# Hybrid attention and convolution layer on one core: a second accumulator bank, output weights in sixteen pieces, a reordered last tile, and side work placed behind the scores

## The chip, the cores and the metric

The kernel runs on one core of one Trainium2 chip. The metric is device time in microseconds (us); lower is better. Three runs of the kernel before gave 764.88, 765.08 and 765.8 us, so its median is 765.08 us.

## The reference

```python
h = rms_norm(x, norm_w)
proj = einsum('bsd,de->bse', h, w_in)
q, kv_all, gate_logits, nsa_z, cv_h, cv_b, cv_c, cv_z = split(proj)
# 8 heads x 64, 2 key groups, three branches, each a masked softmax over its own keys
o_cmp = softmax(q k_c) v_c      # 64 compressed blocks (a small MLP over 32 tokens each)
o_slc = softmax(q k_s) v_s      # all causal tokens: 16 blocks of 64 are all selected at SEQ = 1024
o_win = softmax(q k_w) v_w      # sliding window of 512
o_nsa = (g0 * o_cmp + g1 * o_slc + g2 * o_win) * silu(nsa_z)
u = cv_c * cv_h
o_conv = cv_b * (causal_conv_3(u) + conv_b) * silu(cv_z)       # 512 channels
out = x + concat([o_nsa, o_conv]) @ w_out                      # 1024 x 1024
```

SEQ is 1024 and the model width 1024, all in float32. The kernel keeps float32 accuracy by splitting both operands of a product into a high part in the type fp32r and a rest, and takes three products of 128 x 128 by 128 x 512 (`three`: high x high, high x low, low x high).

## The kernel before, in words

The first 200 us or so normalise x, and project queries, keys, values and a part of the gates. The change doesn't touch them. After that one loop over 136 steps (numbered k, in the code `for k in range(STEPS)`) interleaves two streams of work on TensorE.

**The attention stream.** A unit is a query tile i (128 queries, i = 0 to 7) and a key group g. It has two jobs, the selected branch ("s", even jobs) and the window branch with the compressed one ("w" and "c", odd jobs), and each job has four heads, so there are 128 score steps. Step k writes, at its end, the scores of step k+1 (`scores`, lines 1260 to 1285) into one of two tiles `sc[k % 2]` of two banks each. It must wait until the exponentials of step k-1 have been read from that tile (`exp_done`). VectorE takes the row maxima (lines 1095 to 1099), ScalarE the exponentials (779 to 784), VectorE, ScalarE and GpSimd scale by gate and sum. From step 4n+5 on, the probabilities of job n are transposed on TensorE (`turn`, line 1401), ScalarE casts them to a high part (`pth`, 794), VectorE takes the rest (`ptl`, 1106), and the products with the values follow one turn later (`flush`, 1381 and 1382). The rows grow with i, from 128 to 1024 columns. Every eight steps the next unit's queries are transposed (1249) and split (704, 966).

**The side stream.** It has 52 groups of eight parts, one part being three products of 512 columns. Groups 0 to 35 compute the gate and convolution channels (kinds z, ch, cc, cb, cz, each for two column halves); groups 36 to 51 are the output projection, two for each query tile. Before, all groups but the last accumulate in one bank, `pf`. A group's first part waits until the one before has been read from `pf` (`f_free`, an ordinary counter). How it is read depends on the kind: z is a tanh on ScalarE (762) and then a product on VectorE (1044); ch is a copy on ScalarE (765); cc is a product on VectorE (1052), and after its second half a pass of ScalarE over 1024 columns (768) and two of VectorE (1068, 1069, `convolve`); cb is a product on VectorE (1056); cz is a tanh and two VectorE instructions (1059, 1061); an output group is added to x (1115) and stored.

**The order.** `SIDE` says for each step how many parts lie in its first and in its second group of parts. One step on TensorE is: first turn (or flush), first group of parts, second turn, second group of parts, scores of k+1, queries. The other engines walk through the same steps in the same written order, so an instruction that waits holds up all that stands behind it on its engine.

**The output weights.** w_out (1024 x 1024) is loaded by SP in eight pieces of 128 x 1024 into two buffers `wor0` and `wor1`, cast by ScalarE (831), and its rest taken by GpSimd for even pieces (565) and by VectorE for odd ones (1155), in steps 88 to 91. The last channel part stands in step 87, step 88 has no parts, and steps 89 to 92 have one part in each group. An output part needs its piece (`wol_ready`).

**The last tile.** Query tile 7's output, parts 400 to 415, takes four parts of column half 0, four of half 1, and the same again with the attention half of the mix, which ScalarE casts (837) and GpSimd takes the rest of (570) once both key groups are done.

Of the kernel before, what the change touches and what calls it, by code (L numbers as in the profile page):

```python
# [15 lines left out]
P = 128  # L16
# [71 lines left out]

def win_column(i):
    return 512 - min(i, WT) * P  # L90
# [26 lines left out]

SIDE = [(2, 2)] * 34 + [(2, 1), (2, 1), (2, 0)] * 18 + [(0, 0)] + [(1, 1)] * 4  # L120
# [36 lines left out]

OUT_0 = 8 * NF
# [26 lines left out]
def mixn_half_at(k):  # L185

    for m in range(NT):
        if step_of(OUT_0 + 16 * m + (4 if m == LAST else 0)) == k:
            return m
    return None  # L190
# [5 lines left out]

def wout_at(k):

    return [j for j in range(NK) if WOUT_STEP + j // 2 == k]
# [16 lines left out]
def hybrid_layer(nc: bass.Bass, x, wpack, wside, wout, normw, qnorm, knorm, par, const, maskc, out):  # L216
    with ExitStack() as ctx:
# [26 lines left out]
        with ExitStack() as c:  # L244
# [21 lines left out]
            with ExitStack() as d:  # L266
                wor = [sb("wor0", [P, DM], F32, d), None]
                msh = sb("msh", [P, NK, P], F32R, d)
                msl = sb("msl", [P, NK, P], F32R, d)
                wor[1] = sb("wor1", [P, DM], F32, d)  # L270
# [9 lines left out]
                with ExitStack() as f:  # L280
                    xo = [sb(f"xo{s}", [P, 512], F32, f) for s in range(2)]
# [35 lines left out]
        f_done, f_free, f_tanh, cz_done = sem("f_done"), sem("f_free"), sem("f_tanh"), sem("cz_done")  # L317
        conv_first, conv_done = sem("conv_first"), sem("conv_done")
        wor_in = [sem(f"wor_in{s}") for s in range(2)]
        woh_ready = sem("woh_ready")  # L320
        wol_ready = [sem(f"wol_ready{s}") for s in range(2)]
# [6 lines left out]
        msh_ready, msl_ready = sem("msh_ready"), sem("msl_ready")  # L328
        out_done, out_ready, mixc_used = sem("out_done"), sem("out_ready"), sem("mixc_used")
# [63 lines left out]
        def side_bank(x):  # L393

            return sc[0][:, 0:512] if x == NX - 1 else pf[:, :]
# [14 lines left out]
        def _(sp):  # L410
# [50 lines left out]
            for j in range(NK):  # L461
                output_weights(j)
                if j == 1:
                    sp.wait_ge(conv_done, 4)
                    for c in range(2):
                        residual(c)
# [12 lines left out]
        def _(pool):  # L479
# [66 lines left out]
            for k in range(STEPS):  # L546
# [33 lines left out]
        def _(act):  # L580
# [171 lines left out]
            def side(f):  # L752
# [3 lines left out]
                if kind in ("z", "cz"):  # L756
                    act.wait_ge(f_done, f + 1)
                    if kind == "cz":
                        before = 2 * t + f % 2
                        if before:  # L760
                            act.wait_ge(cz_done, before)
                    A(th[:, :], pf[:, :], ACT.Tanh, scale=0.5).then_inc(f_tanh, 1)
                elif kind == "ch":
                    act.wait_ge(f_done, f + 1)
                    nc.scalar.copy(mixc[:, t, cols], pf[:, :]).then_inc(f_free, 1)
                elif kind == "cc" and f % 2 == 1:
                    act.wait_ge(f_free, f + 1)
# [3 lines left out]
            def exponentials(s):  # L771
# [9 lines left out]
                else:  # L781
                    A(cmp_probs(i, h), sc[s % 2][:, 640:704], ACT.Exp,
                      bias=nmax[:, s % 4, 1:2], accum_out=psums[:, s % 4, 1:2])
                    A(win_probs(i, h), sc[s % 2][:, win_column(i):512 + P], ACT.Exp,
# [15 lines left out]
            for k in range(STEPS):  # L800
# [27 lines left out]
                for j in wout_at(k):  # L828
                    act.wait_ge(wor_in[j % 2], 16 * (j // 2 + 1))
# [656 lines left out]
```

## Time and profile before

| | before |
|---|---|
| median of three runs | 765.08 us |
| profiled execution | 767.03 us |
| its span in the trace | 765.2 us |
| TensorE busy | 702.6 us (92%) |
| VectorE, ScalarE, GpSimd busy | 459.1, 372.9, 189.1 us |
| mean granted TensorE clock | 0.986 |

The span is the time from the first to the last instruction of the profiled execution; 1.8 us more lie around it. TensorE is busy nearly all the time, so a gain has to come from the moments in which it is idle, or runs at a lower clock. The end of a matmul in the trace is modelled: a product of 512 columns is shown with 0.39 us, yet the next one starts 0.23 us later. Start times are therefore the better measure.

### The profile page before, as it was taken

To read this page: it belongs to the slowest core of one execution; us is meant where nothing else is said; L and a number is where in the kernel's file an instruction comes from. 1 tells how busy PE (TensorE), PEld (TensorE's weight loads), DVE (VectorE), ACT (ScalarE), POOL (GpSimd) and SP (SyncE) were. 2 spreads that over 40 slices of the span, in tenths; PEclk is the share of its full clock that TensorE was granted. 3 is DMA by queue.
4 is the path that set the end of the run, shared out by engine and by line. 5 is a ranking of instruction groups with operands and counts; after the bars stand their busy time and mean duration, and the time that the engine had idled before them with its cause. 6 is when DMAs were issued, how large, how long until landed. Compare 5 with 4: busy or idle time off the path is not lost.

```text
span 765.2 us, 10923 instructions
## 1 busy us (share of the span) xinstructions
PE 702.6 (92%) x3951; PEld 588.7 (77%) x3951; DVE 459.1 (60%) x957; ACT 372.9 (49%) x896; POOL 189.1 (25%) x209
## 2 busy tenths in 40 slices
PE   1989999799989999999999999999779999999997
PEld 1878899698768778877877787787557878887775
DVE  3777453734333644567568666687657676776742
ACT  4552525432333434446555555555565555555541
POOL 2112545320223222132122122120341121202120
PEclk9999999999999999999999999999979999999999
DMA  6521131201111101110111000002131111110101
GB/s 207 166 84 28 31 108 38 80 1 42 29 41 42 29 27 42 29 42 15 28 28 28 15 29 28 14 4 80 55 110 42 43 41 42 35 50 28 56 28 56
DMA packets 18053, 36.75 MB, mean 48 GB/s; under 512 B 2512, under 2 KB 3408, under 8 KB 18000
## 3 DMA queue, kind: packets, MB, share of 16 engines
q1 hardware_dynamic: 18000, 36.05, 15.2%
q8 instruction: 32, 0.52, 0.3%
q14 instruction: 21, 0.17, 0.1%
HBM read 31.85 MB, written 4.19 MB: 47 GB/s over the span
## 4 chain that ended last, share of the span: by engine, by line
PE 70%; DVE 13%; ACT 6%; issue 6%; DMA 4%; POOL 1%; SPq 0%; POOLq 0%; ACTq 0%; DVEq 0%
PE pf L1167 11%; PE pf L1168 10%; PE pf L1169 10%; PE tp L1401 6%; PE pj L1167 5%; PE pj L1168 5%; PE pj L1169 4%; PE po L1381 4%; PE po L1382 4%; PE sc L1258 4%; PE sc L1257 3%; DMA wor<-in_wout 2%; DMA qp<-in_wpack 1%; DVE ptl L1106 1%; DVE wol L1155 1%
## 5 line engine op out<-in xcount | busy, mean ns | idle before, releaser
L794 ACT CAST pth<-tp 128x512 fp32r<-128x512 f32 (+1 forms) x148 | 86.5, 586 | 146.1 <-PE tp L1401 145.9
L1106 DVE TENSOR_TENSOR ptl<-tp,pth 128x512 fp32r<-128x512 f32 (+1 forms) x148 | 101.8, 688 | 53.6 <-ACT pth L794 51.1
L1167 PE MATMUL pf<-hh,fh 128*128 128x512 f32 x288 | 116.8, 406 | 7.6 <-DVE mixn L1044 4.6
L1168 PE MATMUL pf<-hl,fh 128*128 128x512 f32 x288 | 112.7, 391 | 0.0
L1169 PE MATMUL pf<-hh,fl 128*128 128x512 f32 x288 | 112.6, 391 | 0.0
L552 POOL TENSOR_SCALAR qp<-qp,precip,gate 128x64 f32<-128x64 f32 x64 | 39.7, 621 | 215.6 <-DVE precip L1081 215.6
L1401 PE MATMUL tp<-cst,qp 128*128 128x128 f32 (+1 forms) x592 | 90.5, 276 | 1.4 <-issue 1.1
L510 POOL TENSOR_TENSOR fl<-fraw,fh 128x512 fp32r<-128x512 f32 x36 | 46.8, 1299 | 150.1 <-ACT fh L661 150.1
L1167 PE MATMUL pj<-wh,hh 128*128 128x256 f32 (+1 forms) x256 | 75.9, 296 | 6.7 <-POOL wl L493 5.4
L1095 DVE TENSOR_REDUCE nmax<-sc 128x1 f32<-128x128 f32 (+7 forms) x64 | 48.4, 756 | 47.2 <-PE sc L1276 46.9
L1168 PE MATMUL pj<-wl,hh 128*128 128x256 f32 (+1 forms) x256 | 74.2, 290 | 0.0
L1167 PEld LDWEIGHTS pf<-hh,fh 128*128 128x128 f32 x288 | 54.1, 188 | 26.1 <-DVE mixn L1044 5.2
L1169 PE MATMUL pj<-wh,hl 128*128 128x256 f32 (+1 forms) x256 | 74.1, 289 | 0.0
L1401 PEld LDWEIGHTS tp<-cst,qp 128*128 128x128 f32 (+1 forms) x592 | 67.2, 139 | 8.5 <-issue 2.4
L1381 PE MATMUL po<-pth,val 128*128 128x512 f32 x132 | 64.2, 486 | 8.8 <-DVE ptl L1106 5.7
L493 POOL TENSOR_TENSOR wl<-qp,wh 128x512 fp32r<-128x512 f32 (+1 forms) x33 | 45.8, 1414 | 92.2 <-ACT wh L592 92.1
L1169 PEld LDWEIGHTS pf<-hh,fl 128*128 128x128 f32 x288 | 54.1, 188 | 12.2
L1168 PEld LDWEIGHTS pf<-hl,fh 128*128 128x128 f32 x288 | 54.1, 188 | 10.6
L1167 PE MATMUL pf<-woh,msh 128*128 128x512 f32 x120 | 49.8, 415 | 8.1 <-POOL wol L565 6.4
L1087 DVE TENSOR_SCALAR qp<-qp,precip,gate 128x640 f32<-128x640 f32 (+7 forms) x96 | 55.1, 574 | 3.5
L1167 PEld LDWEIGHTS pj<-wh,hh 128*128 128x128 f32 x256 | 50.3, 196 | 9.0 <-issue 7.7
L1257 PE MATMUL sc<-kst,qh 128*128 128x512 f32 (+3 forms) x152 | 52.5, 346 | 1.1 <-DVE ql L966 1.1
(179 smaller groups left out, 1522.0 us busy)
## 6 DMA issues: line engine op xcount, KB each, us to landing
fraw<-in_wside SPq DMA_DIRECT2D x36, 256.0 KB, 2.7
qp<-in_wpack SPq DMA_DIRECT2D x28, 256.0 KB, 3.0
qp<-in_x SPq DMA_DIRECT2D x8, 512.0 KB, 3.4
wor<-in_wout SPq DMA_DIRECT2D x8, 512.0 KB, 4.3
xo<-in_x SPq DMA_DIRECT2D x16, 256.0 KB, 2.7
out<-xo SPq DMA_DIRECT2D x16, 256.0 KB, 2.0
qp<-in_wpack SPq DMA_DIRECT2D x5, 224.0 KB, 2.6
mixc<-in_normw SPq DMA_DIRECT2D x1, 512.0 KB, 7.5
```

Source lines behind the costliest of these rows:

```text
L493: nc.gpsimd.tensor_tensor(wl[e % 2][:, j * w:(j + 1) * w], raw[p % 4][:, 0:w], wh[e % 2][:, j * w:(j + 1) * w].bitcast(F32), ALU.subtract)\
L510: nc.gpsimd.tensor_tensor(fl[h % 3][:, :], fraw[h % 2][:, :], fh[h % 3][:, :].bitcast(F32), ALU.subtract)\
L794: nc.scalar.copy(pth[ptn % 2][0:r, :], tp[tpn % 2][0:r, :]).then_inc(pth_ready, 1)
L1087: V.tensor_scalar(p, p, factor, main, ALU.mult, ALU.mult).then_inc(p_dve, 1)
L1095: V.tensor_reduce(nmax[:, s % 4, 0:1], sc[s % 2][:, o:o + (i + 1) * P], AX.X, ALU.max, negate=True).then_inc(max_ready, 1)
L1106: V.tensor_tensor(ptl[ptn % 2][0:r, :], tp[tpn % 2][0:r, :], pth[ptn % 2][0:r, :].bitcast(F32), ALU.subtract).then_inc(tp_read, 1)
L1167: MM(dst, lh, rh, start=start, stop=False)
L1168: MM(dst, lh, rl, start=False, stop=False)
L1169: return MM(dst, ll, rh, start=False, stop=stop)
L1257: MM(dst, qh[:, h, :], keys, start=True, stop=False)
L1381: MM(po[:, :], v, pth[pt % 2][0:r, :], start=first, stop=False)
L1401: ins = nc.tensor.transpose(tp[tpn % 2][0:r, h * P:(h + 1) * P], src, ident)
```

## The change

- **A second side bank.** Odd groups below group 23 (1, 3, ... 21) accumulate in the upper half of `sc[0]`, a bank of its own, and so does group 51. The window scores of tiles 0 to 2 are moved down into the lower half (`end_column`). Each bank counts its own readers (`f_free[bank]`, `uses`), and a group waits only for the last one in its own bank. The scores of step 52 (`WIDE_STEP`), the first wide window row, wait for groups 21 and 22.
- **The order of a step.** The second group of parts now follows the scores of k+1 instead of standing before them.
- **SIDE.** Full steps (2, 2) go on two steps longer, the channels end in step 86 (first group of parts), the step without parts is 87, and eight steps (88 to 95) with (1, 1) follow in place of four (89 to 92). The number of parts is the same.
- **Output weights.** Sixteen pieces of 128 x 512 in four buffers, two per step in steps 87 to 94; ScalarE casts each and GpSimd takes the rest of each. VectorE has none left. The first residual tiles are loaded after the last channel group.
- **Last tile.** Six parts of column half 0, six of half 1, then the last two of each. The attention half of the mix is cast in two quarters, in steps 131 and 133, and VectorE takes their rest instead of GpSimd.

```diff
+def end_column(i):
+    return 512 if i >= 3 else i * P
 def win_column(i):
-    return 512 - min(i, WT) * P
+    return end_column(i) - min(i, WT) * P
...
-SIDE = [(2, 2)] * 34 + [(2, 1), (2, 1), (2, 0)] * 18 + [(0, 0)] + [(1, 1)] * 4
+SIDE = [(2, 2)] * 36 + [(2, 1), (2, 1), (2, 0)] * 17 + [(0, 0)] + [(1, 1)] * 8
...
+WIDE_STEP = next(k for k in range(NS) if k // 4 % 2 and end_column(UNITS[k // 8][0]) == 512)
+EARLY = (SIDE_AT[2 * (WIDE_STEP - 2)]) // 8
+def bank_of(x):
+    return int(x < EARLY and x % 2 == 1 or x == NX - 1)
+def uses(x):
+    return sum(bank_of(y) == bank_of(x) for y in range(x))
...
     if m == LAST:
-        k, n = part // 8 * 4 + part % 4, part // 4 % 2
+        n, k = (part // 6, part % 6) if part < 12 else ((part - 12) // 2, 6 + part % 2)
...
+LAST_STEPS = (output_step(2 * LAST) + 6, output_step(2 * LAST + 1))
 def wout_at(k):
-    return [j for j in range(NK) if WOUT_STEP + j // 2 == k]
+    return [j for j in range(2 * NK) if WOUT_STEP + j // 2 == k]
+def wout_piece(j):
+    n, k = divmod(j, NK)
+    return KT_ORDER[k], slice(n * 512, (n + 1) * 512)
...
         def side_bank(x):
-            return sc[0][:, 0:512] if x == NX - 1 else pf[:, :]
+            return sc[0][:, 512:1024] if bank_of(x) else pf[:, :]
+        def bank_free(eng, x):
+            eng.wait_ge(f_free[bank_of(x)], uses(x) + 1)
...
             def output_weights(j):
-                k = KT_ORDER[j]
+                k, cols = wout_piece(j)
                 if j == 0:
-                    sp.wait_ge(f_done, NF - 2)
-                elif j == 1:
+                    sp.wait_ge(conv_done, 4)
+                elif j == 2:
                     sp.wait_ge(fl_ready, NHALF)
-                else:
-                    sp.wait_ge(wol_ready[j % 2], j // 2)
-                sp.dma_start(wor[j % 2][:, :], wout[k * P:(k + 1) * P, :]).then_inc(wor_in[j % 2], 16)
+                elif j >= 4:
+                    sp.wait_ge(wol_ready, j - 3)
+                sp.dma_start(wor[j % 4][:, :], wout[k * P:(k + 1) * P, cols]).then_inc(wor_in[j % 4], 16)
...
                 for j in wout_at(k):
-                    if j % 2 == 0:
-                        kt = KT_ORDER[j]
-                        pool.wait_ge(woh_ready, j + 1)
-                        nc.gpsimd.tensor_tensor(wol[:, kt, :], wor[0][:, :], woh[:, kt, :].bitcast(F32), ALU.subtract)\
-                            .then_inc(wol_ready[0], 1)
+                    kt, cols = wout_piece(j)
+                    pool.wait_ge(woh_ready, j + 1)
+                    nc.gpsimd.tensor_tensor(wol[:, kt, cols], wor[j % 4][:, :], woh[:, kt, cols].bitcast(F32), ALU.subtract)\
+                        .then_inc(wol_ready, 1)
...
                 for j in wout_at(k):
-                    act.wait_ge(wor_in[j % 2], 16 * (j // 2 + 1))
+                    kt, cols = wout_piece(j)
+                    act.wait_ge(wor_in[j % 4], 16 * (j // 4 + 1))
                     act.wait_ge(f_done, NF)
-                    nc.scalar.copy(woh[:, KT_ORDER[j], :], wor[j % 2][:, :]).then_inc(woh_ready, 1)
+                    nc.scalar.copy(woh[:, kt, cols], wor[j % 4][:, :]).then_inc(woh_ready, 1)
...
+                if k in LAST_STEPS:
+                    g = LAST_STEPS.index(k)
+                    dve.wait_ge(last_hi, g + 1)
+                    V.tensor_tensor(msl[:, 2 * g:2 * g + 2, :], mixn[:, 2 * g:2 * g + 2, LAST * P:],
+                                    msh[:, 2 * g:2 * g + 2, :].bitcast(F32), ALU.subtract).then_inc(last_lo, 1)
...
+                if k == WIDE_STEP:
+                    bank_free(pe, EARLY - 1)
+                    bank_free(pe, EARLY - 2)
...
-                if k == 0 and f >= 1:
-                    pe.wait_ge(f_free, f)
+                if k == 0 and uses(f):
+                    pe.wait_ge(f_free[bank_of(f)], uses(f))
...
                 for t in turned[1:]:
                     turn(n, *t)
+                if k + 1 < NS:
+                    scores(k + 1)
                 for p in side_parts(k, 1):
                     channels(p) if p < OUT_0 else output(p)
-                if k + 1 < NS:
-                    scores(k + 1)
```

## Rows read from the trace of the kernel before

**Rows 1.** The page, sections 1 and 2: busy time, then 40 equal slices in tenths.

```profile
PE 702.6 (92%) x3951; PEld 588.7 (77%) x3951; DVE 459.1 (60%) x957; ACT 372.9 (49%) x896; POOL 189.1 (25%) x209
...
PE   1989999799989999999999999999779999999997
...
PEclk9999999999999999999999999999979999999999
```

**Rows 2.** TensorE's waits: who waited, for whom, us in total, times, longest.

```profile
PE po L1381 <- DVE ptl L1106: 7.9, 9, 3.6
PE pf L1167 <- POOL wol L565: 6.4, 2, 3.2
PE pf L1167 <- DVE mixn L1044: 4.6, 4, 1.2
...
PE pf L1167 <- DVE th L1059: 1.7, 5, 0.5
```

**Rows 3.** Timeline, group 0 to 1: start, duration, engine, line, operation, [idle before].

```profile
204.97 0.23 PE L1276 MATMUL sc<-maskb 128*128 128x128 bf16 x1
...
206.36 0.50 PE L1167 MATMUL pf<-hh,fh 128*128 128x512 f32 x1 [1.17 <-DVE mixn L1044]
```

**Rows 4.** Timeline: scores, then parts of the same group (209); scores, then a turn (235).

```profile
209.41 0.23 PE L1276 MATMUL sc<-maskb 128*128 128x128 bf16 x1
209.45 0.47 PE L1167 MATMUL pf<-hh,fh 128*128 128x512 f32 x1
...
209.76 0.40 PE L1168 MATMUL pf<-hl,fh 128*128 128x512 f32 x1
...
235.45 0.23 PE L1276 MATMUL sc<-maskb 128*128 128x128 bf16 x1
...
235.52 0.61 PE L1401 MATMUL tp<-cst,qp 128*128 128x128 f32 x4
```

**Rows 5.** Timeline, first convolution: group 7's end, its exponentials, next queries, next unit's scores.

```profile
257.43 0.25 PE L1257 MATMUL sc<-kend,qh 128*128 128x192 f32 x1
...
259.80 0.35 ACT L784 ACTIVATE qp<-sc,nmax 128x128 f32<-128x128 f32 x1
...
264.45 0.68 DVE L966 TENSOR_TENSOR ql<-tp,qh 128x512 fp32r<-128x512 f32 x1
...
265.19 0.39 PE L1257 MATMUL sc<-kst,qh 128*128 128x256 f32 x1 [0.30 <-DVE ql L966]
```

**Rows 6.** Timeline: the last channel group is read (step 87); TensorE's next product with values.

```profile
540.76 0.60 ACT L762 ACTIVATE th<-pf 128x512 f32<-128x512 f32 x1
...
546.43 0.79 PE L1381 MATMUL po<-pth,val 128*128 128x512 f32 x1 [3.60 <-DVE ptl L1106]
```

**Rows 7.** Two stretches: us, busy by engine (instructions), PEclk, DMA share, GB/s.

```profile
556.60:563.00 6.40, 6.34 (x18) 4.78 (x19) 3.85 (x6) 4.66 (x8) 4.48 (x5) 0.50 0.51 164
...
577.00:589.50 12.50, 12.50 (x72) 10.21 (x71) 8.39 (x19) 7.78 (x20) 2.41 (x3) 1.00 0.13 43
```

**Rows 8.** Groups by line and shape: busy us, mean ns | idle before, releaser.

```profile
L510 POOL TENSOR_TENSOR fl<-fraw,fh 128x512 fp32r<-128x512 f32 x36 | 46.8, 1299 | 150.1 <-ACT fh L661 150.1
...
L661 ACT CAST fh<-fraw 128x512 fp32r<-128x512 f32 x36 | 22.4, 621 | 26.7 <-PE pf L1169 26.6
```

**Rows 9.** The tile `wor`: ns minimum/median/maximum, first and last start, forms.

```profile
L565 POOL TENSOR_TENSOR wol<-wor,woh x4: 2343/2362/2387, 547.2 to 568.6; 128x1024 fp32r<-128x1024 f32 x4
L1155 DVE TENSOR_TENSOR wol<-wor,woh x4: 1228/1477/2643, 548.1 to 570.7; 128x1024 fp32r<-128x1024 f32 x4
```

**Rows 10.** Timeline: a GpSimd subtraction and a VectorE scaling at the same time.

```profile
401.17 1.27 POOL L510 TENSOR_TENSOR fl<-fraw,fh 128x512 fp32r<-128x512 f32 x1 [5.87 <-ACT fh L661]
...
401.39 1.33 DVE L1087 TENSOR_SCALAR qp<-qp,precip,gate 128x512 f32<-128x512 f32 x1
```

**Rows 11.** Timeline, last tile: cast of the mix, and the first part that needs it.

```profile
754.25 0.62 ACT L837 CAST msh<-mixn 128x512 fp32r<-128x512 f32 x1 [1.39 <-DVE mixn L1141]
...
756.26 0.50 PE L1167 MATMUL pf<-woh,msh 128*128 128x512 f32 x1 [1.22 <-POOL msl L570]
```

More of the change, by code:

```diff
@@ L185, in mixn_half_at @@
 def mixn_half_at(k):
-    for m in range(NT):
-        if step_of(OUT_0 + 16 * m + (4 if m == LAST else 0)) == k:
+    for m in range(LAST):
+        if step_of(OUT_0 + 16 * m) == k:
             return m
@@ L266, in hybrid_layer @@
             with ExitStack() as d:
-                wor = [sb("wor0", [P, DM], F32, d), None]
+                xo = [sb(f"xo{s}", [P, 512], F32, d) for s in range(2)]
                 msh = sb("msh", [P, NK, P], F32R, d)
                 msl = sb("msl", [P, NK, P], F32R, d)
-                wor[1] = sb("wor1", [P, DM], F32, d)
+                wor = [None, None] + [sb(f"wor{s}", [P, 512], F32, d) for s in (2, 3)]
                 qd = sb("qd", [P, GH, 2, HD], F32, d)
@@ L280, in hybrid_layer @@
                 with ExitStack() as f:
-                    xo = [sb(f"xo{s}", [P, 512], F32, f) for s in range(2)]
+                    wor[0], wor[1] = (sb(f"wor{s}", [P, 512], F32, f) for s in (0, 1))
         with ExitStack() as c:
@@ L316, in hybrid_layer @@
         fh_ready, fl_ready, half_used = sem("fh_ready"), sem("fl_ready"), sem("half_used")
-        f_done, f_free, f_tanh, cz_done = sem("f_done"), sem("f_free"), sem("f_tanh"), sem("cz_done")
+        f_done, f_tanh, cz_done = sem("f_done"), sem("f_tanh"), sem("cz_done")
+        f_free = [sem(f"f_free{s}") for s in range(2)]
         conv_first, conv_done = sem("conv_first"), sem("conv_done")
-        wor_in = [sem(f"wor_in{s}") for s in range(2)]
-        woh_ready = sem("woh_ready")
-        wol_ready = [sem(f"wol_ready{s}") for s in range(2)]
+        wor_in = [sem(f"wor_in{s}") for s in range(4)]
+        woh_ready, wol_ready = sem("woh_ready"), sem("wol_ready")
         qd_ready, qh_ready, kend_ready = sem("qd_ready"), sem("qh_ready"), sem("kend_ready")
@@ L451, in output_weights @@
             def output_weights(j):
[L452 removed]
+                k, cols = wout_piece(j)
                 if j == 0:
[L454 to L455 removed]
+                    sp.wait_ge(conv_done, 4)
+                elif j == 2:
                     sp.wait_ge(fl_ready, NHALF)
[L457 to L461 removed]
+                elif j >= 4:
+                    sp.wait_ge(wol_ready, j - 3)
+                sp.dma_start(wor[j % 4][:, :], wout[k * P:(k + 1) * P, cols]).then_inc(wor_in[j % 4], 16)
+            for j in range(4):
                 output_weights(j)
[L463 to L466, printed above, removed]
+            sp.wait_ge(f_done, NF)
+            for c in range(2):
+                residual(c)
+            for j in range(4, 2 * NK):
+                output_weights(j)
             for c in range(2 * NT):
@@ L757, in side @@
                     act.wait_ge(f_done, f + 1)
[L758 to L762, printed above, removed]
+                    if kind == "cz" and 2 * t + f % 2:
+                        act.wait_ge(cz_done, 2 * t + f % 2)
+                    if kind == "z" and f >= 1:
+                        bank_free(act, f - 1)
+                    A(th[:, :], side_bank(f), ACT.Tanh, scale=0.5).then_inc(f_tanh, 1)
                 elif kind == "ch":
                     act.wait_ge(f_done, f + 1)
-                    nc.scalar.copy(mixc[:, t, cols], pf[:, :]).then_inc(f_free, 1)
+                    nc.scalar.copy(mixc[:, t, cols], side_bank(f)).then_inc(f_free[bank_of(f)], 1)
                 elif kind == "cc" and f % 2 == 1:
-                    act.wait_ge(f_free, f + 1)
+                    bank_free(act, f - 1)
+                    bank_free(act, f)
                     A(mixc[:, t, :], ub[:, 2:2 + SEQ], ACT.Identity, scale=prm[:, P_CW + 3 * t + 2:P_CW + 3 * t + 3],
@@ L1043, in side @@
                     dve.wait_ge(f_tanh, f + 1)
-                    V.scalar_tensor_tensor(mixn[:, t, cols], th[:, :], 1.0, pf[:, :], ALU.add, ALU.mult).then_inc(f_free, 1)
+                    V.scalar_tensor_tensor(mixn[:, t, cols], th[:, :], 1.0, side_bank(f), ALU.add, ALU.mult)\
+                        .then_inc(f_free[bank_of(f)], 1)
                 elif kind == "cc":
@@ L1277, in scores @@
                 else:
-                    o, j0 = win_column(i), max(0, i - WT)
+                    o, e, j0 = win_column(i), end_column(i), max(0, i - WT)
                     if j0 < i:
-                        keys_times(s[:, o:512], kst[:, 1, g, j0 * P:i * P], h, i < WT)
-                    keys_times(s[:, 512:512 + P + CB], kend[:, g, :], h, False)
+                        keys_times(s[:, o:e], kst[:, 1, g, j0 * P:i * P], h, i < WT)
+                    keys_times(s[:, e:e + P + CB], kend[:, g, :], h, False)
                     if i >= WT:
                         MM(s[:, 0:P], identb, farb, start=False, stop=True)
-                    ins = MM(s[:, 512:512 + P + CB], identb, endb[:, i, :], start=False, stop=True)
+                    ins = MM(s[:, e:e + P + CB], identb, endb[:, i, :], start=False, stop=True)
                 ins.then_inc(s_done, 1)
```

49 lines of the change are left out of this document (28 added, 21 removed).

## The prediction

> **What bounds the kernel now.** I read the busy shares first. TensorE is busy 92% of the span, no other engine above 60%, and the slices show where the rest lies: the start, one slice near 540 to 575 us where both its busy share and its clock fall to 7 tenths, and a thin loss elsewhere [rows 1]. The change leaves the first 200 us alone. Then I read TensorE's own list of waits, which gives the thin loss its names: a channel group waiting until VectorE has read the bank (lines 1044, 1059), parts of the output waiting for the rest of w_out, and value products waiting for `ptl` [rows 2]. Last I read the timeline at one instance of each. So TensorE sets the time nearly everywhere after 200 us, and each edit is worth what it takes from, or adds to, the gaps between TensorE's starts.
>
> **Part 1: the second bank.** Between group 0 and group 1 TensorE ends its scores at 204.97 and starts the next part at 206.36, 1.39 us [rows 3]. Where the same order has no change of group the step is 0.04 us [rows 4]. The stall is worth 1.35 us, while the list of waits books 1.17, because matmul ends are modelled. Four z boundaries cost 4 x 1.33 = 5.3 us. The other 18 boundaries up to group 22 cost 0 to 0.7 us each (on line 1059, cz, five waits of 1.7 us in all, [rows 2]), by the same reading of starts 5.7 us. The second bank removes all 22 waits, since the group before the previous one has long been read: -11.0 us. The lower end is what the list of waits books for them, some 7.6.
>
> Part of it comes back. With scores(k+1) before the second group of parts, TensorE reaches them 1.38 us (two parts of six products, 0.23 each) earlier, and after a group has ended, ScalarE must first read that group and then take the exponentials that these scores wait for. For z and ch that is 0.6 us plus 0.5 to 0.9, against 1.38 to 1.74 us of parts and turn on TensorE: nearly hidden, I take +0.5 us in total. For the two convolutions in this stretch it isn't hidden. Group 7's products end at 257.43, its exponentials at 260.15, and the next queries are ready at 265.13 because VectorE is in `convolve` until then; the next unit's scores start right behind, 7.8 us after the group's end [rows 5]. That chain runs on ScalarE and VectorE and doesn't shorten. After the change TensorE has one set of scores and two parts less to do inside it (1.7 us), and must do two parts behind it. Laid out step by step, TensorE passes the end of that step 1.3 us later than before, and 1.4 us later at the second convolution (group 15), the bank waits there not gained. Against the 11.0 us, which counts those four boundaries as gained, this is +3.4 us. The later convolutions keep their cover: 0.
>
> **Part 2: the order costs TensorE something of itself.** Scores end in a bf16 product with the mask. Scores followed by a part cost 0.04 us to the next start and 0.31 us for the part's first product, where 0.23 is usual; scores followed by a turn cost 0.07 us [rows 4]. The new order makes scores, part, turn out of part, scores, turn in each step that has a second group and a turn or queries behind it: 82 steps by SIDE. That is 0.04 + 0.08 - 0.07 = 0.05 us each, 82 x 0.05 = +4.1 us. It could be 0 (if the turn behind the part gains what the part loses) or 0.10 each, 8 us.
>
> **Part 3: the output weights.** Before, from the read of the last channel group (540.76) to the end of step 95 (589.5) pass 48.7 us [rows 6, 7]. TensorE's work in it, at the usual distances, is 16 parts x 0.69 = 11.0, 12 turns with their value products x 0.91 = 10.9, nine scores x 0.78 = 7.1 and one set of queries 0.4, in all 29.4 us. The other 19.3 us are waits (3.60 and twice 3.2 us as the longest, [rows 2, 6]) and the half clock behind each: after such a wait the granted clock reads 0.50 for 3 to 6 us, and TensorE does 18 products in 6.4 us where it does 72 in 12.5 at full clock [rows 7]. That is its 1.2 GHz level instead of 2.4.
>
> After, the last channel group ends one step earlier, so 3.0 us more of TensorE's work (two turns, one set of scores, queries) stand behind that point: 32.4 us of work. The waits that remain: at the drain, ScalarE's tanh, two VectorE passes and the cast of the mix still stand before the exponentials, so the scores of step 88 wait about 1.1 us, the first output part 0.7 (its piece's cast and rest are 0.62 and 1.30 us, [rows 8]) and the next value product 0.5. None is as long as the 3.6 us, so I expect the clock to stay up. Then two pieces per step: ScalarE was busy 7.78 us in the three steps 93 to 95, 2.6 a step [rows 7], and 2 x 0.62 more make 3.8, while TensorE's step with two parts is (12.5 - 2 x 0.69) / 3 = 3.7. GpSimd comes to 2 x 1.30 + 0.8 = 3.4, VectorE 2.8. So ScalarE is level with TensorE for seven steps and lags after steps with two turns: I lay out 3.4 us of small waits. Loads don't matter: 256 KB pieces, four buffers, each asked for two steps ahead. And VectorE's scaling on line 1087 (0.61 us on average) takes 1.33 us when a GpSimd subtraction runs beside it [rows 10]; with GpSimd busy most of each step I add 1.3 us. That gives 32.4 + 2.3 + 3.4 + 1.3 = 39.4 us, against 48.7 + 3.0 = 51.7: -12.3 us. Bounds: -17 if only the drain remains, -8 if the 3.6 us wait and its half clock survive.
>
> The row says more here than the mean: the GpSimd subtraction of 1024 columns takes 2.36 us, VectorE's 1.23 at its fastest and 1.48 in the median [rows 9]. The Trainium skill, "GPSIMD Engine Reference", section 4.1 (Engine selection), says that two-input elementwise work belongs on VectorE, as GpSimd is about twice as slow, and this change does the opposite. The trace agrees with the factor; by that rule the stage would end bound by GpSimd, which is the first rival below.
>
> **Part 4: the last tile.** TensorE stands idle 1.22 us (1.38 by starts) until GpSimd has taken the rest of the attention half [rows 11]. After, 12 parts don't need the last key group, so four more (2.8 us) lie behind the cast at 754.25, and the quarter's cast and rest take about 0.8 us together. The wait goes, and the parts behind it are the same in number: -1.4 us, at worst 0.
>
> **Part 5: where group ends fall.** SIDE moves most channel ends by one step. Four waits of 0.4 to 1.4 us in the steps 60 to 84 came from a group's end standing before `ptl` or before the read of the value product on its engine (of [rows 2], line 1381); I count 3.6 us gone and 1.6 new: -2.0, between +2 and -3.6.
>
> **Sum.** -11.0 + 3.4 + 0.5 + 4.1 - 12.3 - 1.4 - 2.0 = -18.7 us. The profiled execution took 767.03 us, its span 765.2 with 1.8 around it, so a span of 746.5. The median of the runs shown lies 1.95 below the profiled execution; the same difference taken off its 765.08 gives 746.4, and I predict 746.5.
>
> **Rivals.**
>
> - **GpSimd and ScalarE take the weights stage back.** If GpSimd is slowed by its neighbour as VectorE was, whose same instruction took 1.2 times its fastest in the median and 2.2 times at worst [rows 9], say by 1.4, a piece takes 1.8 us instead of 1.3; sixteen make 29 us, 5 us of other work come to it, and eight steps of 3.7 are 30: GpSimd bound, 34 against 30. With ScalarE lagging as well, TensorE waits some 4 to 7 us more: 752. For it: the equal loads above. Against it: 1.30 us is the mean of 36 of the same form [rows 8], and the four on line 565 hardly differ [rows 9]. Chance 0.17.
> - **The earlier scores wait.** The second bank does nothing but move the wait: TensorE gets past the group's end and stops at the scores, whose exponentials stand behind the same read. Half of the 11 us returns, and the order costs 0.10 us a step instead of 0.05: 746.5 + 4 + 4 = 754.5. For it: the convolution [rows 5]. Against it: in the list of TensorE's waits none stands on an exponential at all. Chance 0.13.
> - **The other side: slower.** One mechanism: the scores stop for the exponentials of step k-1 in every step with a second group, not only behind group ends, because ScalarE's queue runs level with TensorE. It takes 0.23 us more in each of the 82 steps to eat 18.7 us; at 0.25 the time is 767. ScalarE is at 49%, so I give it 0.03.
> - **The weights stage without residue**: all small waits hidden and the alignment good, -17 and -3.6 in place of -12.3 and -2.0: 740. Chance 0.12.
>
> The forecast keeps 0.55. The range 737 to 755 holds the forecast and the first, second and last of these. A difference of 0.2% is about what a measurement of this kernel can tell from none. Faster by more than that 0.95, within it 0.02, slower 0.03.
>
> **What would show each step.** Waits of line 1167's channel parts on VectorE for groups 1 to 22 gone from the list. Starts after the mask product at 0.04 and 0.31 us. The next unit's scores still 7.8 us behind group 7's end, with 2 to 3 us of waits before them. Granted clock 1.0 through the weights stage, and about 39 us from the last channel group's end to the end of step 95. No wait before the last four parts. The prediction is wrong if the clock still halves there, or if scores wait on exponentials outside the convolutions.

## The result, and the profile after

The changed kernel takes 752.88 us (median of four runs, 752.47 to 753.7), against 764.98 us for the kernel before in the same comparison (four runs, 762.55 to 765.8): ratio 0.9848, interval 0.9824 to 0.9873. It is faster by 12.1 us, inside the range forecast, but 6.4 us short of the 746.5 us predicted.

First the page of the changed kernel, the lines that answer [rows 1].

```profile
PE 699.6 (93%) x3951; PEld 582.8 (78%) x3951; DVE 461.3 (61%) x955; ACT 372.8 (50%) x905; POOL 198.1 (26%) x220
...
PE   2899999799999899999999999999899999999997
...
PEclk9999999999999999999998999999999999999999
```

The hole near 540 to 575 us is nearly gone (8 and 9 tenths where it read 7), and its clock is whole again. The one slice whose clock falls to 8 tenths is now at 394 to 413 us; experiment 4 goes there. None of the other engines is near its limit, since VectorE, the busiest of them, stands at 61%. TensorE's waits after 205 us, in the columns of [rows 2]:

```profile
PE po L1434 <- DVE ptl L1158: 5.6, 8, 1.4
PE sc L1308 <- ACT qp L825: 3.2, 4, 1.4
PE sc L1308 <- DVE ql L1014: 2.5, 2, 1.5
PE pf L1218 <- POOL wol L604: 2.1, 3, 1.3
...
PE tp L1454 <- issue: 1.8, 1, 1.8
```

The waits of channel parts on lines 1044 and 1059 have gone and the wait for the weights' rest fell from 6.4 to 2.1 us. Scores that wait for exponentials (line 825) are a new name. One turn waits 1.8 us for a releaser that the list doesn't know ("issue"); before, the longest wait of that kind was 1.1 us. The first is the forecast's, the second isn't.

**One measure for all kernels.** The profiled spans are 765.2 and 750.7 us, 14.5 us apart, more than the medians are, because the part ahead of the loop, which no edit touches, varies by some us from one execution to the next (its end stands at 204.97 and 202.16 us). So I compare the distance in the trace from the first scores' mask product to the start of the last product. Before it is 204.97 [rows 3] to 761.61, 556.6 us. The timeline of the changed kernel:

```profile
202.16 0.23 PE L1330 MATMUL sc<-maskb 128*128 128x128 bf16 x1
...
747.03 0.39 PE L1220 MATMUL sc<-woh,msl 128*128 128x512 f32 x1
```

That is 544.9 us, 11.8 less, in agreement with the medians. Each distance is read from one execution, so differences of a few tenths say little. All kernels by this measure ("usual order" is the scores last in a step, as before):

| kernel | distance | median | ratio to before (interval) |
|---|---|---|---|
| before | 556.6 | 764.98 | 1 |
| changed | 544.9 | 752.88 | 0.9848 (0.9824 to 0.9873) |
| changed, usual order | 534.9 | 744.33 | 0.9714 (0.9681 to 0.9747) |
| changed, one bank | 557.0 | 766.65 | 1.0023 (0.9999 to 1.0047) |
| changed, late convolutions | 540.4 | 749.42 | 0.9788 (0.9757 to 0.9818) |
| before, new order | 569.1 | 778.99 | 1.0165 (1.0118 to 1.0213) |
| before, two banks | 545.9 | 755.50 | 0.9857 (0.9818 to 0.9895) |
| best: changed, usual order, late convolutions | 531.1 | 739.92 | 0.9649 (0.962 to 0.9679) |
| best, VectorE takes odd pieces' rest | 534.7 | 743.43 | 0.9705 (0.9667 to 0.9744) |
| best, last tile as before | 532.7 | 740.92 | 0.9664 (0.9634 to 0.9694) |
| best, eight weight blocks | 542.7 | 750.89 | 0.9807 (0.9784 to 0.983) |
| changed, usual order in twelve steps | 540.0 | 747.39 | 0.9782 (0.9735 to 0.9829) |

### The profile page after: what moved, and what is told of

Its sections match the earlier page's. It is cut to its first block, busy times and chain, and to the rows that moved or that the text cites. A ratio compares the mean times of both kernels' runs of the same rounds, so it can differ in the third digit from the quotient of the medians.

```text
span 750.7 us, 10966 instructions
## 1 busy us (share of the span) xinstructions
PE 699.6 (93%) x3951; PEld 582.8 (78%) x3951; DVE 461.3 (61%) x955; ACT 372.8 (50%) x905; POOL 198.1 (26%) x220
## 4 chain that ended last, share of the span: by engine, by line
PE 76%; DVE 11%; ACT 5%; issue 4%; POOL 2%; DMA 2%; SPq 0%; ACTq 0%; DVEq 0%; POOLq 0%
PE pf L1218 10%; PE pf L1220 9%; PE pf L1219 9%; PE tp L1454 7%; PE po L1434 5%; PE pj L1218 5%; PE pj L1219 5%; PE pj L1220 5%; PE sc L1308 4%; PE sc L1309 4%; PE po L1435 4%; PE sc L1218 3%; PE sc L1220 3%; PE sc L1219 3%; DVE ptl L1158 1%
## 5 line engine op out<-in xcount | busy, mean ns | idle before, releaser
L1218 PE MATMUL pf<-hh,fh 128*128 128x512 f32 x200 | 85.2, 426 | 0.6 <-DVE ub L1101 0.6
L1454 PEld LDWEIGHTS tp<-cst,qp 128*128 128x128 f32 (+1 forms) x592 | 71.2, 138 | 18.7 <-issue 3.3
L1219 PE MATMUL pf<-hl,fh 128*128 128x512 f32 x200 | 79.1, 395 | 0.0
L1220 PE MATMUL pf<-hh,fl 128*128 128x512 f32 x200 | 79.0, 395 | 0.0
L1138 DVE TENSOR_SCALAR qp<-qp,precip,gate 128x640 f32<-128x640 f32 (+7 forms) x96 | 58.5, 609 | 3.5
L1146 DVE TENSOR_REDUCE nmax<-sc 128x1 f32<-128x128 f32 (+7 forms) x64 | 48.3, 754 | 12.7 <-PE sc L1330 12.5
L1309 PE MATMUL sc<-kst,ql 128*128 128x512 f32 (+3 forms) x152 | 52.4, 347 | 0.0
L1435 PE MATMUL po<-ptl,val 128*128 128x512 f32 x132 | 52.1, 395 | 0.0
L1219 PEld LDWEIGHTS pj<-wl,hh 128*128 128x128 f32 x256 | 49.7, 194 | 0.0
```

What stands on the lines that cost most here:

```text
L1138: V.tensor_scalar(p, p, factor, main, ALU.mult, ALU.mult).then_inc(p_dve, 1)
L1146: V.tensor_reduce(nmax[:, s % 4, 0:1], sc[s % 2][:, o:o + (i + 1) * P], AX.X, ALU.max, negate=True).then_inc(max_ready, 1)
L1218: MM(dst, lh, rh, start=start, stop=False)
L1219: MM(dst, lh, rl, start=False, stop=False)
L1220: return MM(dst, ll, rh, start=False, stop=stop)
L1309: MM(dst, ql[:, h, :], keys, start=False, stop=stop)
```

## The experiments

**1. The order of a step.** Theory: the new order costs time and gives none back. Rival: it is what makes the bank useful. First it is undone alone in the changed kernel (label x1), then done alone in the kernel before (x4).

```diff
-                if k + 1 < NS:
-                    scores(k + 1)
                 for p in side_parts(k, 1):
                     channels(p) if p < OUT_0 else output(p)
+                if k + 1 < NS:
+                    scores(k + 1)
```

> The changed kernel with the second group of parts ahead of the scores again, all else as changed. My theory: the new order costs 0.05 us of TensorE in each of 82 steps (4.1 us), and gives back part of the second bank's gain at the two early convolutions (about 3 us), so this version takes 745 to 747 us, against 752.9. The waits of the scores on ScalarE's exponentials go, and the wait of 1.85 us at step 53 (third convolution) stays, since that comes from where the convolution stands on VectorE. Rival: the earlier scores give the other engines slack that pays for the order; then this version takes 753 to 757 us. Second rival, for step 53 alone: the order causes that wait; then step 53 takes 5.4 us instead of 8.5.

> The kernel before with one edit: the second group of parts follows the scores. My theory: 4.1 us for the switch from mask product to part in 82 steps, 5 to 7 us because the waits at the channel groups' boundaries lose the scores that lay in them, 2 to 3 us at the two early convolutions: 776 to 779 us. Rival: the order is worth something by itself (scores earlier, so more slack for the other engines); then it takes 760 to 768 us.

Measured: 744.33 us and 778.99 us. The second lies in the theory's range, the first 0.7 us below it, so the order costs a little more than the theory had; the rival falls in both. The wait at step 53 stays with the usual order, even longer (2.56 us for 1.85), so the second rival falls as well. By distance the order costs 10.0 us with two banks and 12.5 us with one. In neither does it bring a gain.

**2. The bank.** In the changed kernel all groups but the last go back to one bank (x2, the edit below). In the kernel before the second bank comes alone, by the change's own hunks on `bank_of`, `end_column` and `f_free`, with the order, the side work and the weights as they were (x6).

```diff
 def bank_of(x):
-    return int(x < EARLY and x % 2 == 1 or x == NX - 1)
+    return int(x == NX - 1)
```

> The changed kernel with all side groups but the last in the one bank pf; new order, weights and last tile stay. My theory: the 22 waits at the channel groups' boundaries come back, and each is longer by the scores that no longer lie behind it (0.2 to 0.5 us), less what TensorE spends waiting at the two early convolutions anyway: 13 to 17 us, so 766 to 770 us. Rival: the second bank only moved the wait from the part to the scores; then this version takes 756 to 760 us.

> The kernel before with the second bank alone (steps of fewer than eight groups): order, side work and weights as before. Theory: the waits for the bank at the group boundaries of the first 23 groups go, 11.0 us in the sum of the prediction, and the first two convolutions, which then run with less time ahead of them, take part of it back: 764.9 - 8 to 10 = 755 to 757 us. Rival: the bank brings nothing without the new order, because the side group between a mask product and the first part moves the wait to the scores or to the mask product: 762 to 765 us.

Measured: 766.65 us, and 755.5 us. The bank is worth 10.7 us by distance in the usual order (556.6 to 545.9) and 12.1 us in the new one (557.0 to 544.9). The second figure is too low, because the changed kernel's profiled execution holds a stretch at half clock that the one-bank kernel's doesn't (experiment 4); the medians are 13.8 us apart. The bank doesn't need the new order. What it removes is seen in the waits of TensorE from 205 to 320 us, first before:

```profile
PE pf L1167 <- DVE mixn L1044: 4.6, 4, 1.2
PE pf L1167 <- DVE th L1059: 0.9, 2, 0.5
PE pf L1167 <- DVE ub L1052: 0.5, 1, 0.5
PE pf L1167 <- DVE mixc L1056: 0.4, 1, 0.4
PE sc L1257 <- DVE ql L966: 0.3, 1, 0.3
```

and before with two banks, where the scores' wait for the next queries at the two early convolutions (1.0 us each) is all that is left. With one bank these two are 0.3 us, in the list above, and 0.8 us at 329.62, behind its end; so the two convolutions take back 0.9 us even in the usual order:

```profile
PE sc L1287 <- DVE ql L992: 2.0, 2, 1.0
```

**3. Where the order's cost sits.** The changed kernel with the usual order in steps 12 to 17 and 28 to 33 alone (x10), the steps around the first two convolutions.

```diff
+                early = not (12 <= k < 18 or 28 <= k < 34)
-                if k + 1 < NS:
+                if early and k + 1 < NS:
                     scores(k + 1)
                 for p in side_parts(k, 1):
                     channels(p) if p < OUT_0 else output(p)
+                if not early and k + 1 < NS:
+                    scores(k + 1)
```

> The changed kernel with the old order in twelve of its steps alone, 12 to 17 and 28 to 33, around the first two convolutions. It tests where the new order costs its 8.5 us: in waits at the early convolutions, or evenly. Theory: the waits there fall by 1.8 and 2.0 us (as they did with the old order everywhere), and twelve switches at 0.04 us each go: 752.9 - 4.3 = 748.6 us, 748 to 749.5. Rival: the cost is even over the 82 steps that have a second side group, so twelve of them give 8.5 x 12 / 82 = 1.2 us: 751 to 752 us.

Measured: 747.39 us. Its profiled execution was 7.0 us above that median and its first scores start late (208.92 us against 202.16 in the changed kernel), ahead of all edits, so the distance is the number to read: 540.0, 4.9 less than the changed kernel. The theory holds: twelve of 82 steps carry half of the order's 10.0 us. TensorE's waits from 202 to 325 us in the changed kernel:

```profile
PE sc L1308 <- DVE ql L1014: 2.5, 2, 1.5
PE sc L1308 <- ACT qp L825: 2.4, 2, 1.4
```

and with the usual order in those twelve steps, from 209 to 330 us, since this execution runs 7 us later:

```profile
PE sc L1308 <- DVE ql L1014: 2.0, 2, 1.0
```

**4. The later convolutions.** In the changed kernel the third and fourth convolution on VectorE come one step later (x3).

```diff
-                if k - 1 in CONV_STEPS:
-                    convolve(CONV_STEPS.index(k - 1))
+                for t in range(4):
+                    if k == CONV_STEPS[t] + (2 if t >= 2 else 1):
+                        convolve(t)
```

> The changed kernel with the third and fourth convolution one step later on VectorE (step 52 and 76, where they were before the change), the first two as they are. My theory: SIDE moved these two convolutions to the step before a job's last scaling, so that the scaling and the turn of step 53 wait behind 3.3 us of convolution, TensorE stands for 1.85 us, and its clock halves after it. Undone, step 53 takes 5 to 6 us instead of 8.5 and the kernel 748 to 750 us. Rival: the new order is the cause, and this version takes 752 to 754 us.

Measured: 749.42 us; by distance 4.5 us less. The timeline of VectorE in the changed kernel shows where the turn's wait comes from: two convolution passes of 1.28 us stand in its queue ahead of the last scaling of the job (line 1138).

```profile
393.07 1.33 DVE L1138 TENSOR_SCALAR qp<-qp,precip,gate 128x512 f32<-128x512 f32 x1
394.32 1.27 DVE L1119 SCALAR_TENSOR_TENSOR mixc<-ub,prm,mixc 128x1024 f32<-128x1024 f32 x1
395.63 1.28 DVE L1120 SCALAR_TENSOR_TENSOR mixc<-ub,prm,mixc 128x1024 f32<-128x1024 f32 x1
...
398.34 0.55 DVE L1138 TENSOR_SCALAR qp<-qp,precip,gate 128x512 f32<-128x512 f32 x1
```

The turn on TensorE starts at 398.99, 0.10 us behind that scaling's end. Its line names no releaser ("issue"); that it waited for the scaling is read from the written order and that distance. The turn's row:

```profile
398.99 0.86 PE L1454 MATMUL tp<-cst,qp 128*128 128x128 f32 x4 [1.85 <-issue]
```

The clock halves behind it, as the stretch of the changed kernel shows (columns of [rows 7]):

```profile
399.00:406.00 7.00, 7.00 (x22) 5.40 (x23) 3.56 (x11) 2.44 (x8) 0.39 (x1) 0.52 0.00 0
```

With the convolutions one step later the scaling comes first, and the turn doesn't wait. VectorE's timeline in that kernel:

```profile
397.17 0.55 DVE L1138 TENSOR_SCALAR qp<-qp,precip,gate 128x512 f32<-128x512 f32 x1
397.63 1.28 DVE L1119 SCALAR_TENSOR_TENSOR mixc<-ub,prm,mixc 128x1024 f32<-128x1024 f32 x1
```

The same place now runs at full clock, 31 instructions in 7 us where the changed kernel does 22:

```profile
398.00:405.00 7.00, 5.89 (x31) 4.48 (x30) 6.85 (x14) 3.60 (x9) 0.39 (x1) 1.00 0.00 0
```

By the starts 3.9 of the 4.5 us are won here and 0.6 around the fourth convolution. The wait and the half clock can be told apart, because the one-bank kernel of experiment 2 has the same wait without a fall of the clock:

```profile
413.58 0.63 PE L1454 MATMUL tp<-cst,qp 128*128 128x128 f32 x4 [1.86 <-issue]
...
413.60:420.60 7.00, 6.46 (x34) 5.10 (x35) 5.44 (x14) 3.60 (x9) 0.98 (x2) 1.00 0.01 2
```

Behind this turn the same products take 2.1 us less there than in the changed kernel. So the wait costs about 1.8 us and the half clock about 2.1 us.

**5. Both together** (x5: the edits of experiments 1 and 4).

> The changed kernel with its two faults undone together: the scores of the next step stand last in a step again, as before, and the third and fourth convolution of the side work are due one step later. Alone the first gave 744.3 us and the second 749.4 us, against 752.9 us for the changed kernel (8.6 and 3.5 us less). Theory: the two causes are separate (a switch cost and the waits of the first two convolutions on one side, the turn of step 53 on the other), so they add: 752.9 - 8.6 - 3.5 = 740.8 us, 739.5 to 742. Rival: the late turn of step 53 is worth less with the old order, since the waiting scores no longer stand in front of it; then 743 to 744.5 us.

Measured: 739.92 us, the fastest of all. The two add up within 1 us in the medians; by distance the second is worth 3.8 us here and 4.5 us beside the new order.

**6. Who bounds the weights stage.** In the best kernel VectorE takes the rest of the odd pieces (x7); GpSimd keeps the even ones (`wout_at(k)[:1]`, not shown).

```diff
+                for j in wout_at(k)[1:]:
+                    kt, cols = wout_piece(j)
+                    dve.wait_ge(woh_ready, j + 1)
+                    V.tensor_tensor(wol[:, kt, cols], wor[j % 4][:, :], woh[:, kt, cols].bitcast(F32), ALU.subtract)\
+                        .then_inc(wol_ready[1], 1)
```

> As the kernel with old order and late convolutions, but in the stage of the output weights VectorE takes the rest of every odd piece from GpSimd (the cast that took about twice as long there). It tests whether GpSimd bounds that stage, as one rival of the prediction had it. Theory: the stage is bound by TensorE's own products, with a clock that stays at 1.00 and waits of 4 to 5 us in all, spread over three causes; the longest wait for GpSimd is 1.3 us, so at most that is saved, and VectorE's own drains give some of it back: within 1 us of the same kernel without the edit. Rival (GpSimd is the bound of the stage): 2 to 4 us less.

Measured: 743.43 us. Neither had it: by distance it is 3.6 us slower. The rival, GpSimd as the bound, falls; so does my "within 1 us". By the starts the 3.6 us arise in two places. The first, 1.2 us, is at the first output part: GpSimd's scaling ahead of its first piece takes 1.25 us beside VectorE's piece (0.73 in the best kernel) and ends 0.10 us behind it, TensorE waits 1.84 us for that piece (1.32 in the best kernel), and the clock halves behind the wait, which it doesn't in the best kernel (all four executions have a mean clock of 0.991 to 0.995, those of the best kernel 0.998):

```profile
530.04 1.25 POOL L593 TENSOR_SCALAR qp<-qp,precip,gate 128x64 f32<-128x64 f32 x1 [1.58 <-DVE precip L1133]
530.50 0.69 DVE L1208 TENSOR_TENSOR wol<-wor,woh 128x512 fp32r<-128x512 f32 x1
...
532.57 0.55 PE L1225 MATMUL pf<-woh,msh 128*128 128x512 f32 x1 [1.84 <-POOL wol L605]
...
533.00:536.50 3.50, 3.50 (x12) 2.85 (x11) 1.06 (x2) 1.64 (x4) 1.00 (x2) 0.53 0.44 152
```

The second, 2.4 us, is at two value products that wait behind VectorE, the later of them 2.00 us. The timeline of GpSimd and VectorE there:

```profile
549.27 0.68 DVE L1208 TENSOR_TENSOR wol<-wor,woh 128x512 fp32r<-128x512 f32 x1
...
552.09 1.29 POOL L605 TENSOR_TENSOR wol<-wor,woh 128x512 fp32r<-128x512 f32 x1 [3.76 <-ACT woh L874]
552.72 1.22 DVE L1208 TENSOR_TENSOR wol<-wor,woh 128x512 fp32r<-128x512 f32 x1
...
557.55 1.48 POOL L615 TENSOR_TENSOR msl<-mixc,msh 128x512 fp32r<-128x512 f32 x1
557.80 1.78 DVE L1208 TENSOR_TENSOR wol<-wor,woh 128x512 fp32r<-128x512 f32 x1
...
561.22 0.50 PE L1441 MATMUL po<-pth,val 128*128 128x512 f32 x1 [2.00 <-DVE ptl L1159]
```

Alone VectorE takes 0.68 us for a piece. In these two cases beside a GpSimd subtraction it takes 1.22 and 1.78, and ends 0.56 or 0.55 us after GpSimd does (553.94 against 553.38; 559.58 against 559.03). That is most of the work of one piece, done after the other engine's end and not beside it.

**7. The sixteen pieces by themselves** (x9: the best kernel with eight blocks of full rows, GpSimd and VectorE by turns, two buffers). Its edit is the reverse of the change's hunks on the weights, in the main:

```diff
-    return [j for j in range(2 * NK) if WOUT_STEP + j // 2 == k]
+    return [j for j in range(NK) if WOUT_STEP + j // 2 == k]
...
-                wor = [None, None] + [sb(f"wor{s}", [P, 512], F32, d) for s in (2, 3)]
+                wor[1] = sb("wor1", [P, DM], F32, d)
```

> As the kernel with old order and late convolutions, but the output weights come in eight blocks of full rows as before: even blocks cast and subtracted by GpSimd, odd ones by VectorE, two buffers. It prices the sixteen pieces by themselves. Theory: in the trace the stage from the last channel group to the end of step 95 took 51.7 us before and 40.2 us after, 11.5 us less, and the waits of TensorE in steps 90 to 95 fell by 10.8 us; nearly all of this is the pieces: 739.9 + 10 to 12 = 750 to 752 us, and the granted clock halves again after the long waits. Rival: a good part came from the side work spread over eight steps instead of four, which stays here: 744 to 748 us.

Measured: 750.89 us, 11.5 us more by distance, so the pieces carry the gain and the spread of the side work little. The run undoes the size of a piece, the engine that takes its rest and the number of buffers together; how the 11.5 us divide among these wasn't measured. Experiment 6 changes the engine alone and costs 3.6 us. TensorE's waits from 528 to 565 us:

```profile
PE pf L1219 <- POOL wol L599: 6.5, 3, 2.5
```

The releaser of the second of them is a rest of 1024 columns, 2.34 us in one instruction (timeline):

```profile
539.61 2.34 POOL L599 TENSOR_TENSOR wol<-wor,woh 128x1024 fp32r<-128x1024 f32 x1 [2.69 <-ACT woh L867]
```

And the clock falls behind the first, which is 2.4 us long (stretch):

```profile
533.50:539.00 5.50, 5.44 (x22) 4.24 (x23) 3.83 (x6) 1.11 (x2) 0.72 (x1) 0.69 0.61 193
```

**8. The last tile** (x8: the best kernel with the last tile's parts, casts and rests as before).

```diff
-        n, k = (part // 6, part % 6) if part < 12 else ((part - 12) // 2, 6 + part % 2)
+        k, n = part // 8 * 4 + part % 4, part // 4 % 2
...
-    for m in range(LAST):
-        if step_of(OUT_0 + 16 * m) == k:
+    for m in range(NT):
+        if step_of(OUT_0 + 16 * m + (4 if m == LAST else 0)) == k:
```

> As the kernel with old order and late convolutions, but with the last tile in the order of the kernel before. Theory: the wait between the last products and the output comes back, the time is 1.4 us more, 1 to 2 us. Rival: the order of the last tile moves nothing that ends last: within 0.4 us.

Measured: 740.92 us, 1.0 us more in the medians and 1.6 us by distance. The wait is back, as long as in [rows 11]:

```profile
731.29 0.50 PE L1208 MATMUL pf<-woh,msh 128*128 128x512 f32 x1 [1.22 <-POOL msl L609]
```

## Why the prediction was nearly right, point by point

The distances split the 11.8 us into three steps. From before to the best kernel it is -25.5. From the best kernel to that of experiment 4 only the new order is added, +9.2 (531.14 to 540.37). From there to the changed kernel the two convolutions come a step earlier, +4.5.

- **Part 1, the second bank.** Forecast -11.0 with the four boundaries at convolutions counted as gained, measured -10.7 with the usual order, from which the convolutions have already taken back 0.9 us (experiment 2). Counted as in the forecast the bank gives some 11.6. Group 1 now starts 0.04 us after the scores, where it took 1.39 us [rows 3]:

```profile
202.16 0.23 PE L1330 MATMUL sc<-maskb 128*128 128x128 bf16 x1
202.20 0.47 PE L1218 MATMUL sc<-hh,fh 128*128 128x512 f32 x1
```

- **What comes back at the early convolutions.** Forecast +3.4, and +0.5 for exponentials elsewhere. Experiment 3 gives 4.9, of which 0.8 us stand in steps 50 to 56 and some 0.5 are the twelve switches: 3.6 us, and 4.5 with the 0.9 us that come back in the usual order too. (The 0.8 us go with the clock, which reads 0.50 for 3 us there in experiment 3, for 6 us in the changed kernel.) The bank gave 0.6 more than forecast and 1.1 more came back, so the two errors partly cancel. The form was as laid out too, two waits at each convolution, first for the exponentials, then for the queries, 2.44 us together at the first one and 7.8 us from the group's end still setting the pace as in [rows 5]:

```profile
252.73 0.35 PE L1308 MATMUL sc<-kend,qh 128*128 128x192 f32 x1 [1.37 <-ACT qp L825]
...
257.61 0.39 PE L1308 MATMUL sc<-kst,qh 128*128 128x256 f32 x1 [1.07 <-DVE ql L1014]
```

- **Part 2, the order's own cost.** Forecast 82 x 0.05 = +4.1. What is left of the 10.0 us after the waits is 3.2 us, where waits are the excess of each start-to-start distance over the usual one of the same pair (6.8 us more with the new order): 0.04 us a step. This is an estimate, since it depends on which distance is called usual. Of those 6.8 us the convolutions take 3.3 to 3.8 and the longer half clock at step 53 some 0.8; the rest are small ones, against 0.5 us forecast. So the order as a whole was forecast at 8.0 and measured at 9.2 beside late convolutions and 10.0 beside early ones.
- **"The later convolutions keep their cover: 0" is the step that failed.** It cost 4.5 us by experiment 4, about 1.8 of them the wait itself and 2.1 the half clock behind it. I had laid out the first two boundaries step by step and passed the later ones over because the scores there have more work ahead of them. That is true, but the edit of SIDE moves the end of group 23 from step 51 to step 50 and its convolution from step 52 to step 51, so that the two passes of 1.28 us come ahead of the job's last scaling on VectorE. The wait is not at the bank and not at the scores, but at the turn of step 53. The move was in my text, under part 5, as a matter of alignment; I had asked of it which waits it shifts on TensorE, and not what else stands at that place in VectorE's queue.
- **Part 3, the output weights.** Forecast -12.3, with 39.4 us from the last channel group's read to the end of step 95. In the trace:

```profile
535.73 0.60 ACT L801 ACTIVATE th<-pf 128x512 f32<-128x512 f32 x1 [1.26 <-PE pf L1220]
...
543.43 0.50 PE L1218 MATMUL pf<-woh,msh 128*128 128x512 f32 x1 [1.32 <-POOL wol L604]
...
575.97 0.60 PE L1454 MATMUL tp<-cst,qp 128*128 128x128 f32 x4
```

  That is 40.2 us against 51.7, -11.5, and experiment 7 gives the same 11.5. The clock stays up, as forecast; the longest wait is 1.32 us:

```profile
531.40:540.00 8.60, 7.55 (x46) 5.99 (x44) 6.34 (x14) 5.41 (x15) 2.17 (x3) 1.00 0.17 61
540.00:560.00 20.00, 17.46 (x94) 13.42 (x95) 15.29 (x25) 15.48 (x33) 16.70 (x16) 1.00 0.34 109
560.00:576.00 16.00, 14.80 (x82) 11.26 (x81) 11.99 (x25) 12.90 (x32) 10.62 (x10) 1.00 0.31 97
```

- **Part 4, the last tile.** Forecast -1.4, measured -1.6 by distance and -1.0 in the medians.
- **Part 5, alignment.** Forecast -2.0. What is left of the -25.5 after -10.7, -11.5 and -1.6 is -1.7. This is a remainder; no run tested it alone.

In sum the gains were forecast at -26.7 and came to -25.5, the order at +8.0 and came to +9.2, and the late convolutions at 0 and came to +4.5. All three missed to the slow side. The time lies in the range because the range reached up to 755 us for two rivals, and neither of their mechanisms came; so far the hit owes something to luck. The prediction had named as a sign of being wrong that scores wait on exponentials outside the convolutions. They do, twice in the weights stage (0.57 us at 540.19, where it had itself put 1.1, and 0.25 us at 574.27); that is too little to matter.

**The rivals.** GpSimd is no bound of the weights stage: in its busiest 20 us it is busy 16.70, but TensorE waited for it 2.1 us in all, and relieving it made the kernel slower (experiment 6). The Trainium skill, "GPSIMD Engine Reference", section 4.1 (Engine selection), gives two-input elementwise work to VectorE because GpSimd is about twice as slow. The trace agrees for one instruction alone (0.68 against 1.29 us). With a GpSimd subtraction beside it the advantage is gone (1.22 to 1.78 us in five cases of six), and experiment 6 shows the opposite choice to be the faster one here. That the earlier scores only move the wait was refuted by experiment 2, except at the convolutions; outside them the scores waited 0.8 us for exponentials in the whole loop. That rival's price was also added up wrongly: half of 11 us is 5.5, of which 3.9 stand in the forecast already, so it gives about 752, not 754.5. That the measured time lies close to 752 is no evidence for it, since the waits it needs aren't there. The slower case needed 0.23 us a step and met 0.04. The case of a stage with no residue (740 us) is met only by the best kernel, by another road.

## What to carry to other kernels

When an edit moves a producer's end by a step, walk the written queue of every engine at that place, not only at the places the edit is about: here 2.6 us of work in front of a 0.55 us scaling made TensorE wait 1.85 us, and with the half clock behind it cost 3.9 us. Test the parts of a change one by one, since a sound bank (10.7 us) and sound weight pieces (11.5 us) had carried an order that cost 10.0 us. And issue scores, or whatever waits on a long chain, as late as their consumers allow: in this kernel, with one bank and with two, they gained nothing from standing earlier.

## What the runs showed of the hardware

- **VectorE and GpSimd exclude each other on two-input work.** In all six cases of experiment 6 in which a VectorE piece started inside a GpSimd subtraction, it ended 0.54 to 0.61 us after GpSimd's end, whether it had started 0.25 or 1.22 us behind GpSimd's start. The one that started latest began only 0.07 us ahead of GpSimd's end and took 0.68 us, as alone. It works the other way too: GpSimd's scaling at 530.04 took 1.25 us for 0.73 and ended 0.10 us behind VectorE's piece. The Trainium skill, "SBUF — State Buffer", section "Who interferes with whom", calls the pair's shared port an exclusive lock that is held for a whole instruction, and these ends agree with it: a shared bandwidth would have stretched each by a share of the overlap. In the prediction I had priced it as a mild slowing of VectorE by 1.3 us in the stage, from one instance [rows 10].
- **The length of a wait doesn't settle what the clock does.** I had tied the half clock to waits like the 3.6 us of [rows 2]. Behind the 1.85 us of step 53 the granted clock read 0.52 for 7 us, its 1.2 GHz level, and behind the 1.84 us of experiment 6 it read 0.53 for 3.5 us. But behind the 1.86 us of the one-bank kernel it stayed at 1.00, 2.4 GHz, and so it did behind the 2.00 us at 561.22 in experiment 6. Behind the 1.32 us of the weights stage it stayed at 1.00 as well. The one-bank kernel's ten executions fall into two groups by their mean clock, five at 0.998 (764.7 to 766.5 us) and four at 0.993 (768.8 to 771.1 us) with one between, so the same program seems to meet both cases; only one of the ten, of the first group, has a trace. What decides between them no run shows.
